# Five places re-ordered in a two-block float32 layer on one core: first attention, two stage turns, the ends of the second attention, and the MLP

## The reference

```python
def first_block(...):
    h = rmsnorm(x, pre_norm_g[l]);  proj = h @ w_in
    q, k, v, g_a, u_p, g_p = split(proj)
    a = banded_attention(q, k, v, rel_bias, attn_sink[l]) * silu(g_a)
    p = multiscale_pool(u_p, pool_w[l], pool_scale[l]) * silu(g_p)
    x = x + rmsnorm(concatenate([a, p]) @ w_out, post_norm_g[l])

def second_block(...):
    h = rms_norm(x, norm1_g)
    q, k, v, bg, cg, xc = split(h @ w_in)
    y_attn = chunked_relpos_attention(q, k, v, q_norm_g, k_norm_g, rel_bias) @ w_attn_proj
    y_conv = gated_short_conv(bg, cg, xc, conv_w, conv_b) @ w_conv_proj
    g_attn, g_conv = split(sigmoid(h @ w_gate + b_gate))
    x = x + (g_attn * y_attn + g_conv * y_conv) @ w_out
    h2 = rms_norm(x, norm2_g)
    x = x + square(relu(h2 @ w_up)) @ w_down
```

## Time and profile before

| | before |
|---|---|
| median of 3 runs | 2236.73 us (2234.91 to 2237.05) |
| profiled execution | 2238.04 us, its span 2236.2 us |
| mean granted TensorE clock | 0.995 |
| TensorE matmul busy | 2180.0 us, 97% of the span |
| VectorE / ScalarE / GpSimd busy | 1434.8 us (64%) / 862.8 us (39%) / 985.6 us (44%) |
| DMA | 267.17 MB, mean 119 GB/s |

### The profile page before, as it was taken

The page is one execution under the profiler, slowest core; times in us unless marked ns, Lnnn a source line. Parts: engine busy times, 40 slices in busy tenths (PEclk is TensorE's granted clock), DMA queues, the critical chain, the costliest instruction groups (busy, mean ns, idle before and its releaser), DMA issues. The chain is left out here.

```text
span 2236.2 us, 29134 instructions
## 1 busy us (share of the span) xinstructions
PE 2180.0 (97%) x10530; PEld 1813.0 (81%) x10530; DVE 1434.8 (64%) x2460; ACT 862.8 (39%) x1577; POOL 985.6 (44%) x716
## 2 busy tenths in 40 slices
PE   7999999999999999999999999999999999999999
PEld 7788877778887888888888788888878888787887
DVE  6767774516443666666666474332787877899796
ACT  5455524200003555555555221211454545534332
POOL 3231465535543313223131355447465655665554
PEclk9999999999999999999999999999999999999999
DMA  6320114212324323233232364224135445827333
GB/s 224 99 69 27 44 60 167 93 58 77 130 94 138 91 86 109 70 101 90 85 109 66 130 220 174 85 76 169 67 103 170 147 156 187 301 99 250 133 106 119
DMA packets 195545, 267.17 MB, mean 119 GB/s; under 512 B 57897, under 2 KB 113737, under 8 KB 195441
## 3 DMA queue, kind: packets, MB, share of 16 engines
q1 hardware_dynamic: 118272, 189.59, 24.8%
q10 hardware_dynamic: 77168, 76.19, 10.8%
HBM read 190.19 MB, written 83.95 MB: 123 GB/s over the span
## 5 line engine op out<-in xcount | busy, mean ns | idle before, releaser
L159 POOL TENSOR_TENSOR w_hi<-w_raw,zero 128x512 fp32r<-128x512 f32 x216 | 258.7, 1228 | 903.1 <-PE ps L204 779.8
L204 PE MATMUL ps<-a_hi,w_hi 128*128 128x512 f32 x1408 | 546.6, 409 | 9.7 <-PEq L1670 3.2
L204 PE MATMUL ps<-a_hi,w_lo 128*128 128x512 f32 x1408 | 525.8, 394 | 0.0
L204 PE MATMUL ps<-a_lo,w_hi 128*128 128x512 f32 x1408 | 523.5, 392 | 0.0
L204 PE MATMUL ps<-w_hi,a_hi 128*128 128x512 f32 (+1 forms) x1088 | 420.9, 387 | 10.4 <-POOL w_lo L2629 2.8
L204 PE MATMUL ps<-w_hi,a_lo 128*128 128x512 f32 (+1 forms) x1088 | 419.2, 385 | 0.0
L204 PE MATMUL ps<-w_lo,a_hi 128*128 128x512 f32 (+1 forms) x1088 | 418.9, 385 | 0.0
L204 PEld LDWEIGHTS ps<-a_hi,w_lo 128*128 128x128 f32 x1408 | 265.9, 189 | 59.4
L204 PEld LDWEIGHTS ps<-a_hi,w_hi 128*128 128x128 f32 x1408 | 266.4, 189 | 53.9 <-issue 11.8
L204 PEld LDWEIGHTS ps<-a_lo,w_hi 128*128 128x128 f32 x1408 | 267.3, 190 | 42.7
L164 POOL TENSOR_TENSOR w_lo<-w_raw,w_hi 128x512 fp32r<-128x512 f32 x216 | 288.5, 1367 | 4.2
(11 more groups left out here) (257 smaller groups left out, 3498.4 us busy)
## 6 DMA issues: line engine op xcount, KB each, us to landing
w_raw<-in_w_in_dram SPq DMA_DIRECT2D x32, 1024.0 KB, 5.1
mlp_part<-u_parts SPq DMA_DIRECT2D x26, 1024.0 KB, 8.2
feat_fm<-stage ACTq DMA_DIRECT2D x68, 256.0 KB, 2.1
u_parts<-mlp_acc SPq DMA_DIRECT2D x28, 512.0 KB, 2.9
u_parts<-res SPq DMA_DIRECT2D x28, 512.0 KB, 2.7
conv_in<-feat_fm ACTq DMA_DIRECT2D x24, 512.0 KB, 6.0
qkv_tm<-stage_tm ACTq DMA_DIRECT2D x5, 2048.0 KB, 6.9
res<-in_x_dram SPq DMA_DIRECT2D x16, 512.0 KB, 6.6
```

Source lines behind the costliest of these rows:

```text
L159: hi = nc.gpsimd.tensor_tensor(w_hi[slot][:, k:k + 2, :], w_raw[:, k:k + 2, :], zero[:, 0:1].unsqueeze(2).to_broadcast([P, 2, CW]), ALU.add)
L204: last = nc.tensor.matmul(out_of(o), lhs, rhs(o), start=first and n == 0, stop=final and n == 2)
```

## The change

- **First attention.** TensorE: in step 0 half of a fill piece goes ahead of `scores(2)`. ScalarE: `o_low_half` in even steps and `high` in odd steps now stand ahead of `exps(n + 2)`. VectorE: in odd steps `low` stands ahead of `scale(n + 1)`.
- **Mixing stage and its turn.** The two ends of each window mean are done in one strided instruction where there were two (8 instructions fewer in all). `high_p(3)` and `low_p(3)` move behind the turn, as the first work of ScalarE and VectorE in `phase_norm`; TensorE waits for them ahead of its second weight chunk, SyncE ahead of the fifth row load.
- **Start of the second attention.** The 2 MB store's issue moves behind the turn, directly ahead of the loads of head 0, which go ahead of the gains. The rounds of head 0 follow products 1 and 2 (before: 0 and 1), and ScalarE takes `product_out` ahead of `round_hi`.
- **End of the second attention.** The wait for the last stores moves from ahead of the turn to the start of ScalarE's program in `phase_merge`.
- **MLP.** Group 0: VectorE does `up_sum("m7")` ahead of `operand_low(1, "m6")`, and `up_sum("m2")` of the next group directly behind `add(0, 1)`; ScalarE does `up_high(1, "m2")` ahead of `finish(0, 1)`. Coming down: SyncE issues `load_part(s + 2)` ahead of the part stores of steps 5 and 7.

```diff
@@ -330,6 +330,8 @@
         def _(act):
+            for ready in feat_stored:
+                act.wait_ge(*ready)
             act.dma_start(cw[:, :, :], io["conv_w_2"]).then_inc(c_par, 16)
@@ -504,6 +506,7 @@
         dst_v = dst.rearrange("(t p) n -> p t n", p=P)
+        unstored = []
@@ -563,10 +566,18 @@
                     act.wait_ge(ev_tm, j * (8 * per) + (c0 * 8 + 8 * per + 8))
-                act.dma_start(dst_v[:, :, bass.ds(col, width)], stage[:, q, :, :]).then_inc(st_tm[q], 16)
+                if normed:
+                    act.dma_start(dst_v[:, :, bass.ds(col, width)], stage[:, q, :, :]).then_inc(st_tm[q], 16)
+                else:
+                    unstored.append((dst_v[:, :, col:col + width], stage[:, q, :, :], st_tm[q]))
             each_chunk(act, chunk)
...
             act.wait_ge(*stored)
+    def last_store(act):
+        (to, tile, done), = unstored
+        act.dma_start(to, tile).then_inc(done, 16)
+    return last_store
@@ -851,11 +862,14 @@
             for n in range(STEPS + 1):
+                g0, g1 = (group_end(n - 1), group_end(n)) if n < STEPS else (0, 0)
+                middle = (g0 + g1) // 2
+                if n == 0:
+                    fill(g0, middle)
                 if n + 2 < STEPS:
                     scores(n + 2)
-                g0, g1 = (group_end(n - 1), group_end(n)) if n < STEPS else (0, 0)
-                middle = (g0 + g1) // 2
-                fill(g0, middle)
+                if n:
+                    fill(g0, middle)
                 if n % 2 == 0 and n >= 2:
@@ -962,11 +976,13 @@
             for n in range(-1, STEPS + 1):
+                if n % 2 == 0 and n >= 2:
+                    o_low_half(n // 2 - 1)
+                if n % 2 and 0 <= n < STEPS:
+                    high(n)
                 if n + 2 < STEPS:
                     exps(n + 2)
-                if n % 2 == 0 and n >= 2:
-                    o_low_half(n // 2 - 1)
-                if 0 <= n < STEPS:
+                if n % 2 == 0 and 0 <= n < STEPS:
                     high(n)
@@ -1105,11 +1121,13 @@
                     largest(n + 2)
+                if n % 2 and n < STEPS:
+                    low(n)
                 if n + 1 < STEPS:
...
                     o_add(n // 2 - 1)
-                if 0 <= n < STEPS:
+                if n % 2 == 0 and n < STEPS:
                     low(n)
@@ -1267,7 +1285,6 @@
             high_p(2)
-            high_p(3)
@@ -1297,10 +1314,11 @@
                     dve.wait_ge(par, 48)
-                link(nc.vector.tensor_tensor(y[:, 0:8], summed[:, 0:8], inv[:, g, 0:8], ALU.mult))
-                link(nc.vector.tensor_tensor(y[:, T - 8:T], summed[:, T - 8:T], inv[:, g, 8:16], ALU.mult))
-                link(nc.vector.tensor_tensor(y[:, 0:8], y[:, 0:8], u[:, i % 2, 8:16], ALU.subtract))
-                link(nc.vector.tensor_tensor(y[:, T - 8:T], y[:, T - 8:T], u[:, i % 2, T:T + 8], ALU.subtract))
+                def ends(row):
+                    return row.rearrange("p (a n) -> p a n", n=8)[:, 0:T // 8:T // 8 - 1, :]
+                link(nc.vector.tensor_tensor(ends(y[:, :]), ends(summed), inv[:, g, :].rearrange("p (a n) -> p a n", n=8), ALU.mult))
+                link(nc.vector.tensor_tensor(ends(y[:, :]), ends(y[:, :]), ends(u[:, i % 2, 8:8 + T]), ALU.subtract))
                 nc.vector.scalar_tensor_tensor(y[:, 8:T - 8], summed[:, 8:T - 8], 1.0 / w, u[:, i % 2, 16:T],
@@ -1348,12 +1366,19 @@
             gated(3)
-            low_p(3)
-    return opened
-def phase_norm(name, out_start, opened, x_src, gain, post_gain, x_dst, next_dst, next_col):
+    def last_high(act):
+        nc.scalar.activation(a_hi[:, 4 + order[3], :], res[:, 4 + order[3], :], ACT.Copy).then_inc(hi_p, 1)
+    def last_low(dve):
+        dve.wait_ge(hi_p, 4)
+        nc.vector.tensor_tensor(a_lo[:, 4 + order[3], :], res[:, 4 + order[3], :],
+                                a_hi[:, 4 + order[3], :].bitcast(F32), ALU.subtract).then_inc(lo_p, 1)
+    return opened, (last_high, last_low, (lo_p, 4))
+def phase_norm(name, out_start, opened, x_src, gain, post_gain, x_dst, next_dst, next_col, last_high, last_low, last_row):
@@ -1401,6 +1426,8 @@
                     load_weights(sp, O + 3, O + 4)
+                if t == 4:
+                    sp.wait_ge(*last_row)
                 if t >= 4:
@@ -1472,6 +1499,7 @@
             pe.wait_ge(split_done, O + 2)
+            pe.wait_ge(*last_row)
             for t in range(NT):
@@ -1544,6 +1572,7 @@
+            last_high(act)
             for t in range(NT):
@@ -1618,6 +1647,7 @@
+            last_low(dve)
             dve.wait_ge(gain_in, 32 if post else 16)
@@ -1815,8 +1845,8 @@
                 product(w_start, x - EARLY, range(KB), x)
-                if x < 2:
-                    round_(0, x)
+                if x in (1, 2):
+                    round_(0, x - 1)
             pe.wait_ge(lo_r, 3)
@@ -1879,19 +1909,21 @@
+            last_store(act)
             for ready in ready_first:
                 act.wait_ge(*ready)
+            load_head(0)
             for j in range(2):
...
             act.wait_ge(ext2_st, 64)
-            load_head(0)
             load_bias(0, 0)
-            act.wait_ge(const_ok, 1)
             v_high(0, 0)
             for r in range(2):
-                round_hi(0, 0, r)
                 product_out(0, r - EARLY)
                 product_store(0, r - EARLY)
+                if r == 0:
+                    act.wait_ge(const_ok, 1)
+                round_hi(0, 0, r)
             act.wait_ge(lo_r, 3)
@@ -1963,8 +1995,6 @@
                     product_store(pairs - 1, x)
-            for s in range(2):
-                act.wait_ge(st_h[s], 16 * (4 * pairs + EARLY // 2 + 1))
@@ -2065,6 +2095,8 @@
             pair_loop(dve, body)
+    return [(st_h[s], 16 * (4 * pairs + EARLY // 2 + 1)) for s in range(2)]
@@ -2563,17 +2595,17 @@
                 p, g, h = of(s)
+                if s + 2 == 14:
+                    sp.wait_ge(u_st, 112 * GROUPS)
+                if s >= 3 and s + 2 < ND:
+                    sp.wait_ge(u_lo, SPLIT_UP + 4 * s)
+                    load_part(s + 2, row_in[s % 3].sem)
                 if s == 5:
...
                         store_part(GROUPS - 1, q)
-                if s + 2 == 14:
-                    sp.wait_ge(u_st, 112 * GROUPS)
-                if s >= 3 and s + 2 < ND:
-                    sp.wait_ge(u_lo, SPLIT_UP + 4 * s)
-                    load_part(s + 2, row_in[s % 3].sem)
                 if p == "m6":
@@ -2767,6 +2799,13 @@
                     finish(0, 0, tile)
+                    act.wait_ge(mm_p, 5)
+                    act.wait_ge(combined, 6)
+                    up_high(1, "m2")
+                    finish(0, 1, tile)
+                    act.wait_ge(mm_p, 6)
+                    up_high(1, "m4")
+                    finish(0, 2, tile)
                 else:
@@ -2776,7 +2815,7 @@
                         up_high(i, "m7")
-                if not last:
+                if not first and not last:
                     finish(i, 1, tile)
@@ -2784,7 +2823,7 @@
                     finish(i, 2, tile)
-                else:
+                elif last:
                     act.wait_ge(combined, i * 5 + 3)
@@ -2849,22 +2888,27 @@
                     operand_low(0, "m1")
-                    operand_low(1, "m6")
-                add(i, 0, tile)
+                else:
+                    add(i, 0, tile)
                 dve.wait_ge(w_ready, i * 7 + 3)
...
                 if first:
+                    operand_low(1, "m6")
+                    add(0, 0, tile)
                     operand_low(2, "m7")
                 add(i, 1, tile)
-                if not first:
+                if first:
+                    dve.wait_ge(b_in, 32)
+                    up_sum(nc.vector, "m2")
+                else:
                     part_sums(i - 1, ("m6", "m7"), quarters(i - 1))
...
                 add(i, 3, tile)
-                if not last:
+                if not first and not last:
                     dve.wait_ge(b_in, i * 16 + 32)
                     up_sum(nc.vector, "m2")
-                else:
+                elif last:
                     staged_low(0, range(4))
@@ -2931,14 +2975,14 @@
 phase_first()
-opened = phase_mix()
+opened, last_of_mix = phase_mix()
 o_mem.close()
-stored2 = phase_norm("n2", W_OUT1, opened, x_in, io["norm1_g_2"], io["post_norm_g"], x1, qkv2, 2048)
-phase_tm(W_QK2, [(4, 0, True), (1, 2560, False)], qkv2, stored2)
-phase_attention(8, qkv2, 0, 1024, 2048, 4, ext2, (io["q_norm_g_2"], io["k_norm_g_2"]), W_BCX2, feat2,
-                [(st_tm[0], 16 * tm_stores[0]), (st_tm[1], 16 * (tm_stores[1] + 1))],
+stored2 = phase_norm("n2", W_OUT1, opened, x_in, io["norm1_g_2"], io["post_norm_g"], x1, qkv2, 2048, *last_of_mix)
+last_store = phase_tm(W_QK2, [(4, 0, True), (1, 2560, False)], qkv2, stored2)
+feat_stored = phase_attention(8, qkv2, 0, 1024, 2048, 4, ext2, (io["q_norm_g_2"], io["k_norm_g_2"]), W_BCX2, feat2,
```

(3 more changed lines are left out.)

4 lines of the change are left out of this document (2 added, 2 removed).

## The result

The changed kernel took 2221.08 us in the median of four runs (2219.2 to 2221.67) beside 2236.89 us before: 0.9930 of it, with a 95% interval of 0.9917 to 0.9944. It is faster by 15.8 us (0.7%), where 25.9 were forecast, and the time lies 1.1 us above the forecast's range of 2204 to 2220. Run again beside the experiments, the same kernel gave medians of 2216.5 and 2220.1 us; its 14 runs in all lie between 2214.0 and 2222.1 (mean 2218.7), the 48 of the kernel before between 2231.7 and 2240.4 (mean 2236.0). A slow spell means here a stretch in which the granted clock is 0.50.

A forecast was written before the change was run, and what follows sets the result against it. TensorE's matmuls, 2180.0 of 2236.2 us, were taken as the bound, leaving 56 us of idle time and its slow clock. Terms of 5.1 + 2.7 + 0.5 + 3.1 + 4.7 + 5.9 + 3.9 = 25.9 us gave 2211 us, range 2204 to 2220.

The forecast's parts named there:

- First attention, 5.1 us: Waits for `low` in the first attention: 6.9 us less 3 x 0.6 won; fill piece ahead of `scores(2)` 0.
- The three losses of 0.6 us: First attention: at three waits behind a q split, the exponential ahead of `high` delays the split by up to 0.6 us.
- Turn from the mixing stage, 2.7 us: Turn from the mixing stage: 0.98 us of wait and a slow spell of 1.72 us go.
- covered by TensorE's first 24 matmuls: Behind the mixing-stage turn: the moved pair's 1.1 + 1.2 us hides behind 5.6 us of TensorE work.
- Into the second attention, 0.5 us: Turn into the second attention: the store's issue, 0.39 us, leaves the path, winning about 0.5 us; the spell stays.
- head 0, 3.1 us: Second attention's start: load wait and spell, 4.6 us, go; a new wait of about 1.5 us (7.7 against 6.0) comes.
- Out of the second attention, 4.7 us: Turn out of the second attention: TensorE starts 1.7 us earlier after a 1.5 us wait; 3.04 us of spell goes.
- MLP's first group, 5.9 us: MLP's first group: 4.2 us from unit m2 starting earlier plus 1.7 us of slow clock won.
- Coming down, 3.9 us: Step 9 coming down: its load goes out over 20 us earlier, so 2.20 us of wait and 1.72 of clock go.
- The clock: All TensorE: a wait of about 2 us or more also costs 1.7 to 3.0 us of slow clock; shorter ones none.
- the first (spells stay or come elsewhere, 2215): Waits shorten, but the spell stays behind the turn out of the second attention or comes elsewhere: about 2215 us, chance 0.20.
- The rival on the slow side: First attention: the new order costs each pair of steps, 37.8 us over 32 pairs, giving 2254 us; chance 0.03.

The follow-up runs named there:

- the experiment: Changed kernel with the first attention's rows in the old order (fill piece, high, low and scale): median 2224.50 us, span less spells 2217.0.
- two experiments: Changed kernel with head 0's first two transpose rounds behind products one and two again: 2224.33 us; with head 1's loads behind the third product's copy and store: 2217.06 us.

## Why the prediction was right or wrong

The forecast of 25.9 us had 16.0 us of waits and 9.9 us of clock. Against it stand 13.7 us of waits (2224.4 less 2210.7, the mean of the three profiles) and, as means over all runs, 3.8 us of clock: before, 2236.0 - 1.8 outside the span - 2224.4 = 9.8 us were lost in spells, after 2218.7 - 2.0 - 2210.7 = 6.0. So **the clock is the larger miss** (6.1 us of 8.4), the waits the smaller (2.3). One thing blurs this split: the spell at 677 us in the kernel before stands in the product ahead of the wait of 2.91 us, which was 5.28 where no spell stood there, so the 2224.4 may be up to 1.7 us too low. That would make the waits' miss smaller and the clock's larger.

The small miss in waits is in part luck. The turn from the mixing stage and the way down gave 1.2 and 3.1 us less than forecast, and the first attention gave some 2.5 us more.

- *First attention, 5.1 us.* TensorE's wait of 1.35 us behind it ends at 256.05 us before and at 249.97 after, 6.1 us earlier, although the changed kernel had lost 1.7 us in a spell at 59. In its two repeats, without that spell, it ends at 247.97 and 247.81. With the spell and the different starts taken off, 7.4 to 7.7 us were won (6.3 by the experiment, with its caution above). The three losses of 0.6 us did not come, and 1.7 to 1.9 us of it were no idle time before but matmul time at full clock, which the table of waits does not count; what made that time is not shown. The fill piece at 0: right.
- *Turn from the mixing stage, 2.7 us.* The wait became 1.20 us and the clock 1.00, as forecast, and 1.1 to 1.4 us of the 2.7 were left at the end of the stage. The step "covered by TensorE's first 24 matmuls" failed: it was true for TensorE and false for GpSimd, whose split ran beside the moved pair and ended 1 us later; the wait for the normed rows grew from 1.69 us to between 2.6 and 3.1, which also hangs on when the next weights land.
- *Into the second attention, 0.5 us, and head 0, 3.1 us.* 0.49 us; 2.91 gone and 1.49 come, in the repeats 1.74 and 1.56 (the prediction's own 7.7 less 6.0 is 1.7, where it said about 1.5). Right in each wait, with the cause at head 0 shown by two experiments.
- *Out of the second attention, 4.7 us.* 1.75 us of wait, as forecast; no profile of 15 had a spell behind the 1.47 us.
- *MLP's first group, 5.9 us.* Of 2.79 and 1.96 us 0.54 was left: the waits are right.
- *Coming down, 3.9 us.* Step 9's wait went as forecast, and step 8 got one of 3.07 us. The step "its landing no longer decides: 2.20 + 1.72" failed: the landing no longer decided at step 9, but nothing in the step asks what GpSimd and VectorE do beside each other once their starts move by 0.3 us, so in waits 0.9 us were lost where 2.2 were to be won.
- *The clock.* This is the step that failed by most. The forecast took each wait of about 1.9 us or more as a spell, each shorter one as none, from one profile. In the first profile of the changed kernel all five spells that were to go did go from their places; three came behind waits that had none before. In the 16 profiles of the changed kernel and its variants, behind the waits past the first 40 us:

| wait, us | waits | with a spell |
|---|---|---|
| 1.2 to 1.49 | 78 | 5 (all at 58 us) |
| 1.5 to 1.81 | 23 | 2 (both at 56 to 57 us) |
| 1.82 to 1.93 | 35 | 19 |
| over 2.4 | 27 | 17 |

So the short waits are nearly free, as I had it; but a wait of 1.83 to 3.3 us has its spell in little over half of the cases, and those terms deserved little more than half their size. These are no independent draws: six of the seven profiles with a spell at 56 to 59 us have one at 364 to 374 too, and none of the nine others. The profile of the kernel before shows none behind its 1.82 us at 456, and at the same place 7 of 16 profiles have one. The prediction quoted the Trainium skill, "TensorE: Matmul & The Clock Gate", Part 1, for this: how many matmuls run slow differs from run to run of one kernel. The traces agree: three profiles of the changed kernel had four, one and one spells. I made it a rival at 0.20 where it belonged in the sum.

Of the rivals, the first (spells stay or come elsewhere, 2215) is what happened, together with two mishaps that none named, at the turn from the mixing stage and on the way down. The rival on the slow side was not seen.

Open: why the spells at 58 us come behind a wait of 1.37 us when at other places none does; and what decides between turns and VectorE's run, since at 1962 us VectorE started first and they took turns, and with the sums one step later GpSimd began 0.15 us first at one place (2030.95 against 2031.10) and still took 9.85 us for its four pieces.

## What to carry to other kernels

A wait removed is worth about its length, unless another wait behind it takes it up, and its slow clock only as often as several runs of the same kernel show it; a profile is one draw. Before work is moved behind a turn, ask which engine it will run beside, not only whether TensorE has enough to do meanwhile. Read what a part of a change won from the time at which TensorE gets past the stage, spells taken off, and not from its brackets alone (7.4 to 7.7 us here, where the brackets had 5.9). When a wait ends on GpSimd, compare the same group's duration in both profiles (7.6 or 11.8 us here): if it differs, look at what VectorE does in the same stretch and who started first.

## What the runs showed of the hardware

- VectorE and GpSimd, both reading two tiles in SBUF: either they take turns (VectorE's 1024-column sums 2.3 us each and its 512-column ones 1.2, GpSimd's pieces 1.4 to 2.3), or VectorE runs at its own speed (1.17 and 0.62) and GpSimd's one piece takes 5.74 us. A difference of 0.33 us in the starts changed the one into the other, and 0.48 us of memset changed it most of the way back (four pieces in 11.77, 7.60 and 8.35 us). Who starts first does not decide it everywhere: at 1962 us VectorE did, and they took turns.
- The low half of a row, 1024 columns, took 1.23 us with GpSimd idle and 2.04 us beside its split, whose first part took 5.02 us for 4.03.
- A slow spell of TensorE costs 1.7 us, now and then 3.0, and comes or stays away behind one and the same wait. Where another wait follows the slow unit, it costs less: 2.79, 7.75 us from start to start with the spell, 7.71 without.
